# Gate tiles around the scan, and the second half's z beside the first half's routing

## What is computed

```python
u = rmsnorm(h, ln_mix) * valid
z, xs, bs, cs, dt, sb, sc, sx, gates = split(u @ w_in)
y_ssd = ssd_branch(z, xs, bs, cs, dt, ...)    # conv, chunked scan, then y * silu(z), group norm, @ w_out
y_sc = shortconv_branch(sb, sc, sx, ...)
g = sigmoid(gates)
h = h + (g[..., :D] * y_ssd + g[..., D:] * y_sc) @ w_o
u = rmsnorm(h, ln_ffn)
h = h + peer_ffn(u, w_q, sub_keys, expert_u, expert_v)
```

## Time and profile before

| | |
|---|---|
| median of 3 runs | 2977.29 us (2970.0 to 2979.43) |
| the profiled execution | 2977.42 us, span 2975.7 us |
| PE busy | 2387.6 us, 80% |
| DVE busy | 1767.4 us, 59% |
| POOL busy | 1197.7 us, 40% |
| ACT busy | 550.8 us, 19% |
| first scan | 219.9 to 367.9 us of the span |
| first routing | 589 to 717 us |
| second projection | 717.6 to 934.9 us |

### The profile page before, as it was taken

How to read it: one execution, slowest core, us unless ns; L and a number is a source line. 1 busy time by engine, 2 the same in 40 slices (tenths; PEclk the granted TensorE clock), 3 DMA queues, 4 the chain that set the end, 5 groups by cost and what they waited for, 6 DMA issues and landing times. The chain is left out here.

```text
span 2975.7 us, 28189 instructions
## 1 busy us (share of the span) xinstructions
PE 2387.6 (80%) x9836; PEld 1679.8 (56%) x9836; DVE 1767.4 (59%) x3591; ACT 550.8 (19%) x1477; POOL 1197.7 (40%) x1058
## 2 busy tenths in 40 slices
PE   6998899882888878997888673784657999968888
PEld 5846788572664547884653462351535555527665
DVE  3305511168997986574588878886676777611400
ACT  4411310111322211000221112210121111012221
POOL 0000000004775776483467766874543766300000
PEclk9997999996999998998999786896768999988789
DMA  3321143415999999998789999996985999814265
GB/s 147 134 103 76 42 171 142 163 57 220 413 414 363 402 374 409 378 418 341 284 313 328 413 415 353 331 411 263 399 288 210 410 415 415 349 72 167 109 261 213
DMA packets 173229, 832.06 MB, mean 280 GB/s; under 512 B 20880, under 2 KB 21136, under 8 KB 156192
## 3 DMA queue, kind: packets, MB, share of 16 engines
q0 software_dynamic: 147456, 536.94, 46.9%
q1 hardware_dynamic: 25632, 293.33, 24.8%
HBM read 828.09 MB, written 2.10 MB: 279 GB/s over the span
## 5 line engine op out<-in xcount | busy, mean ns | idle before, releaser
L1103 POOL DMA_INDIRECT expert_rows<-in_peer_u,chosen x512 | 630.3, 1231 | 1074.5 <-DVE chosen L1636 684.6
L1103 POOL DMA_INDIRECT expert_rows<-in_peer_v,chosen x512 | 564.0, 1102 | 294.0 <-issue 137.5
L1177 DVE SCALAR_TENSOR_TENSOR expert_rows<-expert_rows,u 128x1024 f32<-128x1024 f32 x512 | 607.6, 1223 | 107.1 <-DMA expert_rows<-in_peer_u,chosen 92.0
L605 PE MATMUL product<-uT,in_slab 128*128 128x272 f32 (+1 forms) x1024 | 240.3, 391 | 77.5 <-DMA in_slab<-in_w_in 77.5
L1137 PE MATMUL expert_sum<-expert_rows,expert_diag 128*128 128x512 f32 x564 | 266.1, 617 | 21.2 <-ACT expert_diag L1124 15.4
L1187 DVE SCALAR_TENSOR_TENSOR h<-expert_rows,expert_coef,h 128x1024 f32<-128x1024 f32 x186 | 239.3, 1287 | 38.3 <-DMA expert_rows<-in_peer_v,chosen 35.3
L605 PEld LDWEIGHTS product<-uT,in_slab 128*128 128x128 f32 x1024 | 193.4, 193 | 109.4 <-issue 77.7
L1187 DVE SCALAR_TENSOR_TENSOR u<-expert_rows,expert_coef,u 128x1024 f32<-128x1024 f32 x181 | 233.1, 1288 | 29.7 <-DMA expert_rows<-in_peer_v,chosen 25.0
L2357 PE MATMUL mlp_up<-mlp_xT,mlp_slab 128*128 128x384 f32 (+1 forms) x1024 | 227.1, 384 | 4.1 <-DMA mlp_slab<-in_w_up 3.3
L2348 PE MATMUL mlp_down<-mlp_slab,upT 128*128 128x512 f32 x512 | 222.0, 592 | 0.0
L2357 PEld LDWEIGHTS mlp_up<-mlp_xT,mlp_slab 128*128 128x128 f32 x1024 | 157.7, 194 | 76.4 <-issue 9.4
(11 more groups left out here) (384 smaller groups left out, 3109.5 us busy)
## 6 DMA issues: line engine op xcount, KB each, us to landing
in_slab<-in_w_in SPq DMA_DIRECT2D x39, 2048.0 KB, 10.7
mix_slab<-in_w_in SPq DMA_DIRECT2D x16, 2048.0 KB, 10.4
mlp_slab<-in_w_up SPq DMA_DIRECT2D x16, 2048.0 KB, 9.3
mlp_slab<-in_w_down SPq DMA_DIRECT2D x16, 2048.0 KB, 9.4
mix_slab<-in_ssd_w_out SPq DMA_DIRECT2D x8, 2048.0 KB, 9.6
out_slab<-in_w_out SPq DMA_DIRECT2D x6, 2048.0 KB, 9.2
expert_rows<-in_w_in SPq DMA_DIRECT2D x4, 2048.0 KB, 7.3
mix_slab<-in_sc_w_out SPq DMA_DIRECT2D x4, 2048.0 KB, 9.5
```

Source lines behind the costliest of these rows:

```text
L605: ins = pe.matmul(bank[n % 4][:, 0:W], slab[s][:, k, c:c + P], uT[:, k, A:A + W], start=k == 0, stop=k == KD - 1)
L1103: pool.indirect_dma_start(out=self.row(n), out_offset=None, in_=self.tables[0 if dot else 1], in_offset=bass.IndirectOffsetOnAxis(ap=picks ...
L1177: dve.scalar_tensor_tensor(self.row(n), self.row(n), 1.0, u, ALU.mult, ALU.mult, accum_out=dot).then_inc(self.rows_used, 1)
```

## The change

- The first two gate slabs are asked for at the end of the first `project` instead of at the start of `scan`. Of the 16 gate tiles three stand on PE ahead of the scan's first sums, ten in steps 0, 1, 3, 4, 6, 8, 9, 11, 12 and 14, and three behind the last step. ACT's drains stand behind the first exponentials, behind Ln, behind the last exponentials of the prologue, in the ten steps, and behind the root.
- z of the second half is computed in the first half's `route`: two matmuls in each of its 16 steps and 32 behind them, in two more PSUM banks, drained by ACT with Copy; its slabs use `lend[6:8]`, the first two loaded behind the query slabs in the `ffn_` norm. In the second `project` remain two Silu operations of ACT over z in place, ahead of `leave`.
- The gather of the ninth expert row (ring row 8) waits until z's eight tiles are done.
- z of the second half has memory of its own; the second routing's first query slab takes that memory over.

```diff
@@ block_one
-                z = sbuf(ctx, "z", [P, TT, INNER])
+                z = z_two[0] if half else sbuf(ctx, "z", [P, TT, INNER])
...
+                    gate_slabs = [] if half else first_slabs("gate", lend[6:8], t["w_in"][in_slab(O_G):in_slab(O_G) + 2])
...
+            if half == 0:
+                z_two.append(sbuf(first, "z_two", [P, TT, INNER]))
...
+                z_slabs = [] if half else first_slabs("z", lend[6:8], t["w_in"][in_slab(O_Z):in_slab(O_Z) + 2])
@@ project: SP, PE, ACT
             slab_loader(sp, [s[:] for s in slab], landed, product, 4,
-                        [(lambda s: w_in[in_slab(O_XS) + s], 8),
-                         (lambda s: w_in[in_slab(O_Z) + s], 4)])
+                        [(lambda s: w_in[in_slab(O_XS) + s], 8)] +
+                        ([] if half else [(lambda s: w_in[in_slab(O_Z) + s], 4)]))
+            for dst, src, in_ in ahead:
+                sp.dma_start(dst, src).then_inc(in_, 16)
...
-            for s in range(INNER // SLAB):
+            for s in range(0 if half else INNER // SLAB):
...
+            for m in range(TT if half else 0):
+                act.activation(z[:, m, :], z[:, m, :], ACT.Silu)
@@ scan
+    EARLY, LATE = (3, 3) if gating else (0, 0)
+        MIDDLE = N - EARLY - LATE
+        gate_step = [n * N // MIDDLE for n in range(MIDDLE)]
...
+            def drain_gate(n):
+                act.wait_ge(gate_done, n + 1)
+                act.activation(gates[n // KD][:, n % KD, :], gate_bank, ACT.Copy).then_inc(gate_used, 1)
...
             act.activation(rate_row[:], rows[:, 1, :], ACT.Exp).then_inc(a_exp, 1)
+            if gating:
+                drain_gate(0)
             for n, (x, y_) in enumerate(each(soft[1], soft[3])):
                 act.wait_ge(one_ready, n + 1)
                 act.activation(y_, x, ACT.Ln).then_inc(log_ready, 1)
+            if gating:
+                drain_gate(1)
...
             act.activation(root[:], ssq[:], ACT.Sqrt, scale=1.0 / GW, bias=eps[:]).then_inc(root_ready, 1)
+            for n in range(N - LATE, N):
+                drain_gate(n)
...
+            def gate_tile(n):
+                pe.wait_ge(gate_in[n // 4 % 2], 16 * (n // 8 + 1))
+                if n:
+                    pe.wait_ge(gate_used, n)
+                for k in range(KD):
+                    ins = pe.matmul(gate_bank, gate_slab[n // 4 % 2][:, k, n % 4 * P:(n % 4 + 1) * P],
+                                    uT[:, k, M:M + TOK], start=k == 0, stop=k == KD - 1)
+                ins.then_inc(gate_done, 1)
+
+            for n in range(EARLY):
+                gate_tile(n)
             pe.wait_ge(adt_ready, SETS)
...
+                if gating and q in gate_step:
+                    gate_tile(EARLY + gate_step.index(q))
...
+            for n in range(N - LATE, N):
+                gate_tile(n)
@@ Experts.start
+                if free and n == self.RING // 2:
+                    pool.wait_ge(*free)
@@ route: SP, PE, ACT
+            for s in range(2, INNER // SLAB if z_part else 0):
+                sp.wait_ge(z_done, TT * (s - 1))
+                sp.dma_start(z_slab[s % 2], t["w_in"][in_slab(O_Z) + s]).then_inc(z_in[s % 2], 16)
...
+            def z_products(first, last):
+                for i in range(first, last):
+                    n, k = divmod(i, KD)
+                    s, m = divmod(n, TT)
+                    if k == 0:
+                        pe.wait_ge(z_in[s % 2], 16 * (s // 2 + 1))
+                        if n >= 2:
+                            pe.wait_ge(z_used, n - 1)
+                    at = META + TOK + m * P
+                    ins = pe.matmul(z_bank[n % 2][:], u_all[:, k, at:at + P], z_slab[s % 2][:, k, :],
+                                    start=k == 0, stop=k == KD - 1)
+                    if k == KD - 1:
+                        ins.then_inc(z_done, 1)
...
                         score_tile(i, j - 1)
...
+                    if z_part:
+                        z_products(Z_STEP * (8 * i + j), Z_STEP * (8 * i + j + 1))
                 score_tile(i, 7)
+            if z_part:
+                z_products(Z_STEP * 16, Z_TILES * KD)
...
+                    if z_part:
+                        drain_z(Z_STEP * (8 * i + j - 1) // KD if 8 * i + j else 0, Z_STEP * (8 * i + j) // KD)
                 drain_scores(i, 7)
+            if z_part:
+                drain_z(Z_STEP * 15 // KD, Z_TILES)
```

More of the change, by code:

```diff
@@ L438, in block_one @@
                 route(frame, slab_loader, ident, xT, slab, chosen[half], weight[half],
-                      state, small.count, bg, [f[2] for f in first[1:]], chosen_ready, keys, keys_in)
+                      state, small.count, bg, [f[2] for f in ahead[1:]], chosen_ready, keys, keys_in,
+                      None if half else (uT, z_two[0], lend[6:8], [f[2] for f in z_slabs], z_two_done))
                 end_stage()
@@ L544, in project @@
 def project(frame, slab_loader, ident, uT, z, xs, xs_meta, bt, bt_meta, bf, cf, dt, constants, carry,
-            buffers, half, bg, constants_in):
+            buffers, half, bg, constants_in, ahead):
     nc, t, sem, sbuf, psum, block, enter, leave, leave_sync = frame
@@ L676, in _ @@
                     drain(n - 3)
-            for n in range(INNER // SLAB * TT):
+            for m in range(TT if half else 0):
+                act.activation(z[:, m, :], z[:, m, :], ACT.Silu)
+            for n in range(0 if half else INNER // SLAB * TT):
                 s, m = n // TT, n % TT
@@ L1004, in _ @@
                     begin(q + 1)
-                if q < N and gating:
-                    pe.wait_ge(gate_in[q // 4 % 2], 16 * (q // 8 + 1))
-                    if q:
-                        pe.wait_ge(gate_used, q)
-                    for k in range(KD):
-                        ins = pe.matmul(gate_bank, gate_slab[q // 4 % 2][:, k, q % 4 * P:(q % 4 + 1) * P],
-                                        uT[:, k, M:M + TOK], start=k == 0, stop=k == KD - 1)
-                    ins.then_inc(gate_done, 1)
+                if gating and q in gate_step:
+                    gate_tile(EARLY + gate_step.index(q))
                 if q < N:
@@ L1085, in row, with start @@
         return self.rows[:, n % self.RING, :]
-    def start(self, half, u, h, chosen, weight, ready):
+    def start(self, half, u, h, chosen, weight, ready, free=None):
         self.halves.append((u, h, weight))
@@ L1445, in route @@
         turned = [psum(ctx, f"keys_turned{i}", [P, 4, P]) for i in range(2)]
+        if z_part:
+            u_all, z, z_slab, z_in, z_done = z_part
+            z_bank = [psum(ctx, f"z_product{i}", [P, 512]) for i in range(2)]
+            z_used = sem("z_two_drained")
+            Z_TILES, Z_STEP = INNER // SLAB * TT, 2
         hit = sbuf(ctx, "hit", [P, SLOTS * TOPK])
@@ L1525, in drain_scores, with drain_z @@
                 act.activation(score[j % 2][:], scores[j % 2][:, 0:TT, :], ACT.Copy).then_inc(scores_used, 1)
+            def drain_z(first, last):
+                for n in range(first, last):
+                    act.wait_ge(z_done, n + 1)
+                    act.activation(z[:, n % TT, n // TT * SLAB:(n // TT + 1) * SLAB], z_bank[n % 2][:], ACT.Copy
+                                   ).then_inc(z_used, 1)
             for i in range(0, 2):
```

35 lines of the change are left out of this document (19 added, 16 removed).

## The result

The changed kernel took 2998.33 us (median of 8 runs, 2988.32 to 3005.16), the kernel before 2974.23 us in the same comparison (8 runs, 2966.49 to 2979.43): ratio 1.0081, 95% interval 1.0063 to 1.0099. It is slower, by 24 us where 11 were forecast. Its median lies 0.3 us above the end of the range, 2998; against the kernel before, which took 3.2 us less here than the 2977.4 of the sum, it is 3.5 us beyond it. The profiled execution took 2997.64 us, 20.2 more than that of the kernel before.

The account below looks back on a forecast made before the run. No engine is busy throughout: PE paces the first half's routing, DVE the second half's projection. Scan -3.1, routing +28.2 and projection -14.2 make +10.9 on 2977.4: 2988 us, range 2973 to 2998.

Parts of the forecast that it names:

- three large terms: The sum's stage terms: first half's scan -3.1 us, its routing +28.2 us, second half's projection -14.2 us.
- the wait behind the first query product: First half's routing: PE wants the first z slab at 595.7 but it lands at 598.1, costing +2.4 us.
- 15 x 1.72 = 25.8: First half's routing: 15 steps of two z matmuls, 1.72 us each, precede tile 14's score, adding 25.8 us.
- the cover of Exp: First half's routing: ACT's Exp behind the last z drain stays hidden, by 1.8 us, before DVE wants it.
- The steps: First half's scan: six of 16 steps lose their gate tile, saving 9.3 us; bounds -20.7 and -5.5.
- The end: First half's scan end: three late gate tiles make PE and ACT, not DVE, end the stage, +3.7 us.
- The projection: Second half's projection: without z's matmuls, drains and slabs it gets 14.2 us shorter; bounds 0 and -45.7.
- a row each 1.27 us: Second projection's left-over dots: DMA brings a row each 1.27 us against 1.146 used; 32 dots cost 3 rows of lead.
- More loss: Rival, chance 0.13: ACT's z drains in the first routing hold up Exp, delaying both halves' expert stream; 2992 to 2997.
- The same balance, smaller: Rival, chance 0.30: full-clock state copies, punctual first z slab, or bare steps gaining more; mostly 2980 to 2986.
- its first condition: Scan prologue, within the smaller-balance rival: state products run at full clock, some 1.3 us apart, saving 3.1 us.

Follow-up runs that it names:

- e5: The changed kernel with z's first two slabs asked for at the end of the first half's merge: 2994.31 us, ratio to the kernel before 1.0083.
- e8: The changed kernel itself, run again unaltered on another chip: 3002.03 us against 2970.36 for the kernel before, ratio 1.0102.
- e7: The changed kernel with all z products behind the routing's steps, only steps 5, 7, 13 bare, no gate tiles behind the loop: 2957.65 us, ratio 0.9952.
- e6: The changed kernel with z's four slab loads put back into the second projection, unused: 3006.56 us, ratio to the kernel before 1.0120.
- e10: e7 with ring rows 8 to 11 freed behind z's sixth tile, plus a one-column DVE memset behind each left-over dot: ratio to the kernel before 0.9989.
- e12: e7 with a one-column DVE memset behind each left-over dot of the second projection: 2959.66 us against 2974.77 for the kernel before, ratio 0.9947.

## Why the prediction was wrong

**The direction and the mechanism were right, and the size was not:** each of the three large terms came out on the costly side.

**The step that failed is the wait behind the first query product, "+2.4 us".** It measured 7.4 (4.4 for the slab, 3.0 for the clock), 5.0 of the 9.3 us by which the profiled pair misses the sum. The slab's time was worked out as if the queue delivered the two z slabs one after the other, the first at 598.1. Both together were there when the sum had them (DMA is busy at 410 GB/s until 602; the sum gives 602.9), but the first was usable only at 599.5, when about two thirds of the bytes of both had moved. PE wanted it at 595.1, 0.6 us earlier than forecast. And the pause was priced at its own length only, though the earlier trace rows showed the scan's state products, between pauses, at half clock. e5 takes the late slab away, and both parts are gone. The rest of the routing held: 15 x 1.72 = 25.8 against 25.5 in e5, the steps 5.62 apart, and the cover of Exp: its table load begins at 717.17, it runs at 718.47, and `chosen` is at 720.33 with no wait. The Trainium skill ("ScalarE: Activation LUTs", What ACT_TABLE_LOAD costs) puts a table switch at 2.66 us, about 1.28 for the load and 1.38 for a drain. The rows show the load, 1.28 us, and no drain: Exp follows its load by 0.02 us.

**The steps, "Sum -9.3 us", were right for one profile (-8.8) and not for most (-4.8 in e8).** Each bare step was costed by its dependencies at full clock. Those hold: 3.8 us for the isolated ones, a wait for `mixer` at 2-3 and 10-11. What was left out is that at these pairs, where a missing tile gained 0.1 us, PE's new idle time (2.8 us in 13) can take the clock: 14.5 us instead of 12.8. The clock fell there in five profiles of eight. e7, which keeps the tiles in these pairs and removes the isolated ones only, has no slow step and gains 6.0 us in the scan.

**The end, "+3.7 us", measured 5.0 to 5.9.** PE waits 1.93 us for DVE ahead of the `yo` of bare step 15, the granted clock is at 0.50 from about 349.7 to 356, and the late tiles begin in that stretch, so tile 13 ends behind the root and not ahead of it. That PE and ACT end the stage was right, and in e7, without late tiles, the stage ends 5.2 us behind the root again.

**The projection, "-14.2 us", measured -12.8 and -8.0.** In the first profile the term itself held: behind the loop it took 13.8 us less than before, with the last dot starting 36.2 us behind the first and no wait, and the loop, taken to be unchanged, took 1.0 us more. Free DMA engines were taken to deliver "a row each 1.27 us", but GpSimd asked for a row each 1.76 us there and each 2.29 in e8. With z's loads gone, the supply is no longer bounded by DMA (224 to 247 GB/s from 925 us on in e8; 402 to 425 between 890 and 930 us in the kernel before) but by GpSimd beside a DVE without gaps; in e8 the lead of 16 rows doesn't last, and the stretch gains 8.5 us. e6 shows the other half: with the loads back, DMA limits the rows, dots stand 1.28 us apart, and no gather takes 1.98 us. e10 to e12 show that DVE's spacing decides which pattern comes: without the memset two dots take 2.29 us, as long as a slow gather and the 0.30 us behind it, so each gather meets its dot at the same point; with it they take 2.31, so the next gather starts earlier against its dot and gets in first. That last step is worked out from the rows, not tried by itself. The Trainium skill ("SBUF — State Buffer", Who interferes with whom) says that a DVE instruction with two SBUF inputs contends with a GpSimd instruction that reads SBUF, and that the order of issue decides which of them stands still. The rows agree: a gather that starts behind the dot stands still until 1.09 us into it (2.03 less 0.94), and one that gets in first costs the dot 0.07 us. Which port it is no run here shows. It should have been weighed in the prediction.

**What the forecast of rivals was worth.** "More loss" (2992 to 2997) came nearest in size, short by 1.3 us, but by luck: it named the wrong place, and Exp stayed covered. "The same balance, smaller" failed on its first condition, the state products: they stay 1.73 us apart. One gap is not closed: the profiled pair differs by 20.2 us, which would lie inside the range, the medians by 24.1 and, on the chip of e8, 31.7. The slow pairs (4 us) and the gathers (5 us) are of that size, but which of the unprofiled runs had them can't be seen.

## What to carry to other kernels

A load that lands late on a busy PE costs more than its lateness (here 4.4 us late, 7.4 lost): count the pause, then the work behind it at half clock, and issue the load a stage earlier if memory allows. Take work out of a step only where the chain behind it gets shorter; where it only turns into idle time on PE, it gains nothing and can cost the clock. Work for an engine is best put where the engine is idle: two matmuls in each step of the routing cost 25.5 us, and z behind the steps nothing up to `chosen`. But look at what then waits for it: the rows that GpSimd may fill only behind z moved the next projection's start by 2.6 us in e7.

## What the runs showed of the hardware that was not expected

- A gather issue on GpSimd takes 0.94 us by itself. Beside a DVE dot of 1.22 us it ends 2.03 us behind the dot's start, wherever in the dot it starts from 0.05 to 1.08 us; if it starts within 0.03 us of the dot's start it takes 0.94 us, and the dot is 0.07 us longer. With dots back to back the two engines lock into step, one gather in two dots (2.29 us), or two in three (3.51 us).
- A DVE memset of one column (0.06 us in the row) behind each dot makes the dots only 0.01 us longer apart, and all three profiles with it show two gathers in three dots. Of the eight profiles in which z's loads are gone and no memset stands behind the dots, one shows that pattern to the end (after) and one in part (e5).
- Of two 2 MB loads that were queued one behind the other on SP's queue, the first was usable only about 2.7 us before DMA fell silent, not 4.9, the time of one slab at 430 GB/s.
- A pause of 4.42 us on PE brought the granted clock from 1.00 to 0.50 while PE stood still. A wait of 2.23 us in a step was followed by such a fall in five profiles of eight with the same gate tiles, and in three it was not.
